# Slot order over the partitions, a later fourth weight load and an earlier residual gather in a mixture-of-experts stage on one Trainium2 core

## What is computed

```python
def _hier_moe(h, ...):                       # h: 1024 tokens x 1024
    g_idx = top 1 of 4 groups                # per token
    e_idx = top 2 of the 8 experts of that group
    for every expert e of the 32:
        hid = silu(h @ w_gate[e]) * (h @ w_up[e])     # 1024 -> 256
        out += (hid * coefficient[token, e]) @ w_down[e]
x = x + out
return rmsnorm(x, final_g)
```

## Time and profile before

| | |
|---|---|
| three timed runs, median (lowest to highest) | 1113.54 us (1113.49 to 1115.85) |
| the profiled execution, its own time | 1113.31 us |
| its span, first to last instruction | 1111.4 us |
| PE, DVE, ACT, POOL busy | 90%, 45%, 25%, 15% of the span |
| HBM read, written | 146.36 MB, 26.29 MB |
| weight loads of the experts | 32 sets of 3 x 1024 KB |

### The profile page before, as it was taken

The page is one execution under the profiler, slowest core; times in us unless marked ns, Lnnn a source line. Parts: engine busy times, 40 slices in busy tenths (PEclk is TensorE's granted clock), DMA queues, the critical chain, the costliest instruction groups (busy, mean ns, idle before and its releaser), DMA issues. The chain is left out here.

```text
span 1111.4 us, 13469 instructions
## 1 busy us (share of the span) xinstructions
PE 1002.5 (90%) x5091; PEld 585.9 (53%) x5091; DVE 498.2 (45%) x1221; ACT 279.2 (25%) x630; POOL 163.7 (15%) x152
## 2 busy tenths in 40 slices
PE   6999999974799989999999999996999988888963
PEld 4434777764555456767667455564454433333421
DVE  3477660059725456766665224274632111111135
ACT  3200011030122377656565011020001100000161
POOL 4000000025301131200110000011211211111222
PEclk9999999986899999999999999996999989899987
DMA  9201020032400091000000242546899999999864
GB/s 253 98 6 39 1 76 1 1 40 79 85 12 1 1 236 75 2 1 2 1 1 1 76 145 102 208 175 235 299 294 356 372 393 397 395 375 396 302 240 163
DMA packets 53922, 164.89 MB, mean 148 GB/s; under 512 B 24634, under 2 KB 26746, under 8 KB 41496
## 3 DMA queue, kind: packets, MB, share of 16 engines
q1 hardware_dynamic: 45184, 144.42, 35.9%
q0 software_dynamic: 8672, 19.61, 6.6%
HBM read 146.36 MB, written 26.29 MB: 155 GB/s over the span
## 5 line engine op out<-in xcount | busy, mean ns | idle before, releaser
L1935 PE MATMUL banks<-shared,wout 128*64 128x512 f32 (+1 forms) x416 | 153.3, 640 | 17.3 <-issue 15.0
L1543 PE MATMUL banks<-wout,shared 128*128 128x512 f32 x256 | 112.7, 594 | 0.5 <-PEq L1206 0.5
L368 PE MATMUL banks<-x,wout 128*128 128x512 f32 x256 | 112.0, 594 | 1.1 <-DVE x L409 1.1
L1935 PEld LDWEIGHTS banks<-shared,wout 128*64 128x64 f32 (+1 forms) x416 | 57.9, 174 | 88.5 <-issue 88.2
L1254 ACT ACTIVATE shared<-shared,low 128x640 f32<-128x640 f32 (+7 forms) x128 | 92.9, 729 | 2.6 <-DVE low L1341 2.1
L1983 DVE SCALAR_TENSOR_TENSOR mix_bt<-mix_bt,slot_coef,banks 128x256 f32<-128x256 f32 x24 | 11.5, 481 | 173.6 <-ACT mix_bt L1963 173.6
L1304 PE MATMUL banks<-consts,shared 128*128 128x128 f32 x528 | 77.8, 282 | 4.4 <-ACT shared L1254 3.6
L368 PEld LDWEIGHTS banks<-x,wout 128*128 128x128 f32 x256 | 47.8, 190 | 60.2 <-issue 58.1
L1304 PEld LDWEIGHTS banks<-consts,shared 128*128 128x128 f32 x528 | 56.0, 140 | 43.8 <-issue 38.2
L1543 PEld LDWEIGHTS banks<-wout,shared 128*128 128x128 f32 x256 | 47.6, 190 | 55.2 <-issue 55.2
L1957 PE MATMUL banks<-shared,hidt 128*64 128x512 f32 (+1 forms) x208 | 72.5, 596 | 1.2 <-DVE wout L2000 1.2
(11 more groups left out here) (358 smaller groups left out, 1287.7 us busy)
## 6 DMA issues: line engine op xcount, KB each, us to landing
shared<-in_exp_w_down SPq DMA_DIRECT2D x26, 1024.0 KB, 18.2
shared<-in_exp_w_gate SPq DMA_DIRECT2D x26, 1024.0 KB, 14.0
shared<-in_exp_w_up SPq DMA_DIRECT2D x26, 1024.0 KB, 24.5
x<-in_exp_w_gate SPq DMA_DIRECT2D x6, 1024.0 KB, 14.5
x<-in_exp_w_up SPq DMA_DIRECT2D x6, 1024.0 KB, 22.1
x<-in_exp_w_down SPq DMA_DIRECT2D x6, 1024.0 KB, 21.5
shared<-in_x SPq DMA_DIRECT2D x8, 512.0 KB, 7.9
wout<-in_w_in SPq DMA_DIRECT2D x2, 2048.0 KB, 8.6
```

What stands on the lines that cost most here:

```text
L368: ins = nc.tensor.matmul(bank[:], slot[:, c, c0:c0 + P], ht[:, c, half * 512:half * 512 + 512], **flags)
L1543: ins = nc.tensor.matmul(psum[n % 4], src[:, i * P:i * P + P], m["wout"][:, k, half * 512:half * 512 + 512], start=k == 0, stop=k == KD - 1)
L1935: ins = nc.tensor.matmul(psum[2 + p][rows].rearrange("p (a f) -> p a f", a=2), xt[:, p, k, rows], wgu[b][:, :, k], start=k == 0, stop=k == ...
```

## The change

Four edits, and a stricter assertion that goes with the last:

- A constant row `slot` is added to the table of constants (128 more columns). Partition q of a pass now holds slot 16 (q mod 8) + 2 ((q mod 64) div 8) + (q div 64). Read the other way, consecutive slots go to partitions 0, 64, 8, 72, 16, 80, ... 56, 120, then 1, 65, 9, 73, and so on.
- In a shared pass the first expert gets the even slots, which are partitions 0 to 63, and the second the odd ones, partitions 64 to 127. The place arithmetic changes: one small DVE instruction more where the shift is set, and three more where the row is formed.
- SP waits for the first two gathers to land before it asks for gate and up set 3; down set 4 stands behind it in the queue.
- POOL issues the residual rows of pass 20 right after scatter 19, ahead of gather 23, and asks only that scatters up to 18 have landed (passes 19 and 20 belong to different halves of the experts).

```diff
+        "slot": np.broadcast_to(16 * (q % 8) + 2 * (q % 64 // 8) + q // 64, (P, P)),
...
         for j in (2, 3):
+            if j == 3:
+                for k in range(2):
+                    sp.wait_ge(m["rows_in"][k], 16)
             load_gate_up(nc, d, m, sp, EXPERT[loads[j][0][1]], buffer_of(j))
...
-            chain.note(V.tensor_tensor(row_hot[:, :, at], bc(ch["pos"][:, :, at], P, 3), bc(bc(m["row"], t1 - t0, 1), 2, 1),
+            chain.note(V.tensor_tensor(row_hot[:, :, at], bc(ch["pos"][:, :, at], P, 3), bc(bc(m["slot"], t1 - t0, 1), 2, 1),
...
-    assert not any(passes[n][2] & passes[n - 1][2] for n in range(first, NP) if n > first)
+    assert not any(passes[n][2] & passes[n - 1][2] for n in range(first, NP))
...
     def residual_rows(gp, n):
-        rows_landed(gp, max(first - 1, n - 2))
+        rows_landed(gp, n - 2)
...
-                if n == first + 1:
-                    residual_rows(gp, first)
+                if n == first:
+                    residual_rows(gp, n)
+                elif n == first + 1:
                     residual_rows(gp, n)
...
-                    V.tensor_tensor(row_hot[:, n:n + 4], bc(c[name][:, n:n + 4], P, 2), bc(m["row"], 4, 1), ALU.is_equal
+                    V.tensor_tensor(row_hot[:, n:n + 4], bc(c[name][:, n:n + 4], P, 2), bc(m["slot"], 4, 1), ALU.is_equal
...
-                ts(by_half(adj)[:, 0], paired[:, 0], -P / 2, ALU.mult)
+                for h in range(2):
+                    ts(by_half(adj)[:, h], paired[:, h], float(h - P), ALU.mult)
...
-                tt(c["adj"], c["adj"], c["main"], ALU.mult)
-                tt(c["row"], c["row"], c["adj"], ALU.add)
+                ts(c["t"], c["adj"], -0.5, ALU.is_lt)
+                tt(c["t"], c["t"], c["q"], ALU.mult)
+                tt(c["t"], c["t"], c["adj"], ALU.add)
+                tt(c["t"], c["t"], c["main"], ALU.mult)
+                tt(c["row"], c["row"], c["t"], ALU.add)
```

## The result

The changed kernel takes 1117.38 us (median of 20 runs, 1113.03 to 1119.63) against 1113.42 for the kernel before on the same chips (20 runs, 1110.69 to 1116.58): a ratio of 1.0033, 95% interval 1.0024 to 1.0041. That is 3.7 us slower (2.7 to 4.6), where 2.8 were forecast.

The account below looks back on a forecast made before the run. The DMA engine moving most rows was taken to bound the expert stage. The terms 4.0 - 1.7 + 0.3 + 0.2 = +2.8 us on 1113.31 gave 1116.1, and 1116.3 as median; range 1111.5 to 1120 us.

Parts of the forecast that it names:

- The fullest engine bounds the stage: Expert stage: the DMA engine moving most rows hardly rests from 775.3 us, working 280 of 286 us to 1061.5.
- Fours, with p and p + 32 together: Row transfers: partitions p to p+3 share a DMA engine with p+32 to p+35, eight engines per half of the partitions.
- Slots spread, +4.0: Passes 16 and 18: the new slot order puts 8 rows, not 4, on the fullest engine; +4.0 us, bounds 0 and 5.6.
- Fourth set later, -1.7: Stage start: gather 0 lands 2.0 us sooner, partly lost to PE's half-speed clock; -1.7 us, bounds -0.4 and -2.7.
- Residual rows sooner, 0: Stage end: PE's 2.37 us wait for pass 20's sum is not decisive; 0 us, bounds -2.4 and +0.3.
- A slower last product, +0.3: Stage end: PE rests longer before the last product, which may run slower at low clock; +0.3 us, up to 2.
- Constants, +0.2: Loading start: the constants grow by 64 KB; +0.2 us, between 0 and 0.25.
- Rival 2: Whole stage: groups of eight partitions share an engine, so the spread works, 20.5 us less engine work; 1092 us; chance 0.08.
- Rival 1: Pass 16 to the x_rows reads: the fullest engine absorbs the extra rows at no cost; 1112.3 us; chance 0.24.
- rival 3: Stage end: pass 20's sum decides, so earlier residual rows give 2.4 us; 1113.6 us; chance 0.06.
- Rival 4: Last 16 weight sets: each waits for one more 8 KB piece on some engine, 5 us more; 1121 us; chance 0.05.
- The sign of the down loads: Stage end: last down loads still taking about 31 us means right; landing within 20 us means wrong, rows balanced.

Follow-up runs that it names:

- slots alone: Kernel before with only the change's slot order, comparisons and place arithmetic: 1119.43 us against 1113.08, ratio 1.0057; repeated: 1118.14 us, ratio 1.0046.
- one engine: Kernel before with two groups of four partitions exchanged in slot order, giving engine 0 192 rows: 1117.54 us against 1113.24, ratio 1.0042.
- fours alone: Kernel before with only a slot order putting any 16 consecutive slots on 16 engines, and its arithmetic: 1103.07 us, ratio 0.9903.
- wait alone: Kernel before with only the fourth weight set asked for after the first two gathers land: 1112.11 us, ratio 0.9995.
- residual alone: Kernel before with only the residual rows of pass 20 issued ahead of gather 23: 1112.60 us, ratio 0.9998.

## Why the prediction was right, point by point

The time lay in the range, and the main mechanism was right. That the sum came within 0.9 us of the measured time is in part luck: slots alone measured 1 to 2 us more than its price, and the start gained about as much less than forecast.

- **The fullest engine bounds the stage.** Right, and shown: one engine's 8 rows moved the whole by 4.7 us (3.1 to 6.2), and the slot order that relieves it takes 1% off. "It hardly rests" was too strong for the first passes: rows taken off there were worth 0.2 us each, not 0.525.
- **Fours, with p and p + 32 together.** Right. The runs of four skipped slots carried the forecast; one engine and fours alone, built on the rule, moved the way it says, one slower and one faster.
- **Slots spread, +4.0.** The mechanism and the two passes were right. Slots alone measured 6.3 and, again, 5.1 us; the same number of rows on one engine 4.7 and on three 2.9. Three of the four intervals hold 4.0, that of the first run begins at 4.5; the margin for eight engines (up to 5.6) may have been needed in part.
- **Fourth set later, -1.7.** The term that was mis-sized. The gather gained 1.0 us, not 2.0; 4.54 us is at the upper end of the earlier trace rows, not at the earlier trace rows, which I had preferred for the short POOL instruction. And the clock rose no earlier than before, the case that I had named at net 1.0 and not taken. The start cost 0.2 us with the whole change, from the gather's issue to the sixth request (17.1 to 17.3); wait alone measured -0.6 (-1.6 to +0.6). The prediction took the clock's rise for something near 770 us; in the traces it came between 767.5 and 770.4, 6.0 to 8.5 us after PE resumed, and what sets it stays open. The two kernels that have both the wait and the order by fours show 1.1 and 1.6 us less at the start, in one execution each.
- **Residual rows sooner, 0.** Right: PE's wait of 2.37 us left without effect. In the changed kernel a wait of 1.85 us for gather 23, which had moved behind them, took its place; the prediction had not seen that wait. It too was hidden.
- **A slower last product, +0.3.** It took 9.21 us, 0.3 less than before, although PE had waited. Wrong in sign and too small to matter.
- **Constants, +0.2.** Not visible: the stages ahead ended a microsecond earlier in this execution (757.19 against 758.19), which is their own spread.
- **The working.** The sum for the fullest engine leaves out the two gathers of residual rows, which were issued at 1054 and 1056 us: 16 rows, up to 2.9 us more. Rival 2 takes 184 rows for the kernel before, which is the count by fours; if eight neighbours shared an engine it would be 192, so that rival stood for 1088 and not 1092. All upper bounds at once give some 1122, not 1121. None of this touches the forecast.

The sum came out 0.9 us short of the measured 3.7. Part by part the runs give 5.1 or 6.3 for the slots, -0.6 for the wait and -0.2 for the residual rows, 4.3 to 5.5 together, with intervals wide enough to hold the 3.7. Rival 1 (rows absorbed) is excluded for slots alone by its interval, rival 2 (eight neighbours) by one engine and fours, and rival 3 by residual alone. Rival 4 had 1121 and is outside the interval of the whole change; the surplus of eight engines over one, 0.4 us by the two ratios taken together, is well below its 5 us.

Of the signs named in advance, three came: the share from 1043 to 1054 us rose (hardly in the mean, 0.61 to 0.63, but clearly from dips of 0.1 to a floor of 0.4), the last down loads kept their 31 us (32.6), PE's waits grew by 2. The sign of the down loads was a poor one: with the rows balanced they still take 29.6 us, and not under 20 as it had it. The fourth read landed at 1073.7 instead of near 1072, and the gather did not come within 3.7 us.

## What to carry to other kernels

A busy share of 1.0 over sixteen DMA engines says nothing of their balance: look for a mean share that falls while loads are still outstanding, and count the work of the one engine that gets most. A partly filled indirect transfer is worth balancing by the true division of partitions among the engines, found here from the runs of skipped slots in the packets; an even-looking stride of eight made it slightly worse, and the order by fours, one constant away from it, gave 1%. And a gain at the start of a stage may be paid back by TensorE's clock, if the clock rises no sooner than before; read where it rises in more than one trace before calling it fixed.

## What was not expected of the hardware

- One engine of sixteen with 8 rows (4 KB each, gathered and accumulated) more than before made a launch of 1113 us 4.7 us longer.
- TensorE's clock stood at half speed until 770 us in both kernels, although PE resumed at 763.8 us before and at 761.8 after; the product that began 2.0 us earlier ended only 0.8 us earlier. In wait alone PE resumed at 760.5 and the clock rose at 767.5.
- The fourth read of `x_rows`, asked for 2.4 us later in residual alone, landed at the same time (1069.01 against 1069.17).
- With the rows balanced over the sixteen engines, the last down loads still took 29.6 us from issue to landing.
